# Stick-breaking prompt attention: the scores' second product with high queries and low keys alone, two query tiles at once in the two halves of the array's rows

## The reference, cut to what matters

```
z = einsum('bqhd,bkhd->bhqk', q, k) * scale          # scores, 64-long products
log_keep = where(causal, log_sigmoid(-z), 0)
after = sum of log_keep over the keys behind this one
a = exp(log_sigmoid(z) + after), 0 where not causal
o = einsum('bhqk,bkhd->bqhd', a, v)
```

## Time and profile before

| | |
|---|---|
| median of 3 executions | 2858.61 us (2857.3 to 2861.83) |
| profiled execution, span from first to last instruction (what is shown of its own time) | 2862.5 us |
| busy: PE, DVE, ACT, POOL | 2813.8, 1649.9, 1317.5, 1155.7 us |
| stage `phase_attend` on TensorE, scores | 1453.6 to 2555.6 us |
| mean granted TensorE clock | 0.992 of full |

### The profile page before, as it was taken

How to read it: one execution, slowest core, us unless ns; L and a number is a source line. 1 busy time by engine, 2 the same in 40 slices (tenths; PEclk the granted TensorE clock), 3 DMA queues, 4 the chain that set the end, 5 groups by cost and what they waited for, 6 DMA issues and landing times. The chain is left out here.

```text
span 2862.5 us, 42044 instructions
## 1 busy us (share of the span) xinstructions
PE 2813.8 (98%) x14856; PEld 2467.1 (86%) x14856; DVE 1649.9 (58%) x2151; ACT 1317.5 (46%) x2733; POOL 1155.7 (40%) x1023
## 2 busy tenths in 40 slices
PE   7999999999999999999999999999999999999998
PEld 6999999999988888889978888888888888878886
DVE  5322132213243350112268999999999999988775
ACT  6000000000043331111157888888888888875542
POOL 3333333333110120002256867676777768651110
PEclk9999999999999999999999999999999999999999
DMA  5101111111064343434687766867767776767873
GB/s 157 38 23 37 38 38 30 32 41 38 13 200 130 122 167 143 169 120 147 186 245 211 228 197 200 243 198 215 220 203 211 237 198 196 218 187 211 238 219 108
DMA packets 280359, 433.33 MB, mean 151 GB/s; under 512 B 52578, under 2 KB 218594, under 8 KB 274180
## 3 DMA queue, kind: packets, MB, share of 16 engines
q1 hardware_dynamic: 269156, 391.41, 45.1%
q0 software_dynamic: 11040, 39.86, 4.7%
HBM read 307.40 MB, written 123.81 MB: 151 GB/s over the span
## 5 line engine op out<-in xcount | busy, mean ns | idle before, releaser
L1981 POOL TENSOR_TENSOR a_a<-a_a,a_prod 128x512 f32<-128x512 f32 (+3 forms) x640 | 661.6, 1049 | 305.3 <-DVE a_prod L1932 183.8
L1932 DVE TENSOR_TENSOR_SCAN a_prod<-a_keep,a_prod,a_restart 128x513 f32<-128x513 f32 x384 | 476.0, 1268 | 30.2 <-ACT a_keep L1876 28.9
L1875 ACT ACTIVATE a_a<-a_pz 128x512 f32<-128x512 f32 (+3 forms) x640 | 358.0, 559 | 58.2 <-PE a_pz L1802 51.6
L1885 ACT ACTIVATE a_ath<-a_pt 128x512 fp32r<-128x512 f32 (+3 forms) x640 | 327.3, 556 | 102.2 <-PE a_po L1816 72.7
L1942 DVE TENSOR_TENSOR a_atl<-a_pt,a_ath 128x512 fp32r<-128x512 f32 (+3 forms) x640 | 359.9, 597 | 18.5 <-ACT a_ath L1885 16.1
L1876 ACT ACTIVATE a_keep<-a_pz 128x512 f32<-128x512 f32 (+3 forms) x640 | 361.6, 566 | 0.0
L1825 PE MATMUL a_pt<-ident,a_a 128*128 128x128 f32 x2176 | 316.9, 275 | 4.5 <-DVE a_atl L1942 2.4
L1825 PEld LDWEIGHTS a_pt<-ident,a_a 128*128 128x128 f32 x2176 | 262.2, 142 | 44.4 <-DVE a_atl L1942 5.0
L1801 PE MATMUL a_pz<-a_kh,a_q 128*128 128x512 f32 (+3 forms) x640 | 255.9, 403 | 3.5 <-ACTq L1866 2.0
L279 POOL TENSOR_TENSOR w_wh<-w_raw,w_gain 128x1024 fp32r<-128x1024 f32 x22 | 41.5, 1889 | 537.0 <-PE v_pg L349 279.9
L1814 PE MATMUL a_po<-a_ath,a_v 128*128 128x512 f32 (+3 forms) x640 | 245.9, 388 | 1.6 <-POOL a_v L1992 0.9
(11 more groups left out here) (233 smaller groups left out, 6165.1 us busy)
## 6 DMA issues: line engine op xcount, KB each, us to landing
a_x<-x_d SPq DMA_DIRECT2D x84, 896.0 KB, 5.7
a_x<-x_d SPq DMA_DIRECT2D x56, 832.0 KB, 4.9
a_kh<-kh_t SPq DMA_DIRECT2D x32, 512.0 KB, 7.0
a_kl<-kl_t SPq DMA_DIRECT2D x32, 512.0 KB, 9.1
w_raw<-in_a_w_in POOLq DMA_DIRECT2D x30, 512.0 KB, 4.8
x<-f_xn POOLq DMA_DIRECT2D x17, 512.0 KB, 5.3
g_y_in<-sz_t SPq DMA_DIRECT2D x17, 512.0 KB, 7.4
g_x<-x SPq DMA_DIRECT2D x17, 512.0 KB, 3.7
```

What stands on the lines that cost most here:

```text
L1875: act.activation(a[:, s, q, 0:w], pz[:, n % ZS, 0:w], ACT.Sigmoid, scale=SCALE)
L1885: act.activation(ath[:, b % AS, c0:], pt[:, turn_slot(pr, hh, b), c0:], ACT.Copy).then_inc(at_hi, 1)
L1932: dve.tensor_tensor_scan(prod[:, s, 0:w + 1][:, ::-1], keep[:, n % KS, 0:w + 1][:, ::-1], restart[:, 0:1].broadcast_to([P, w + 1]), prod[: ...
L1981: pool.tensor_tensor(part, part, prod[:, n % PS, after:after + w], ALU.mult).then_inc(weighted, 1)
```

## The change

For an even query tile only the first product is made at its turn. At the odd tile's turn come its first product and then the second products of both tiles, with 64 rows each: qh of the even tile by kl in one half of the rows, qh of the odd tile by kl in the other. ql·kl is no longer computed. Since both need qh, and `q2` has qh in one half only, a new tile `qx` holds qh of the odd query tiles in the other half; for odd heads the halves of `q2` and `kl2` change places. `qx` is loaded by one more DMA per head (`load_odd`), for the first head at the beginning of the stage on a semaphore of its own. `prod` goes from 8 slots to 6, its slots now count through all pieces, and each scan waits for the scan two pieces before it. The planner's costs follow.

```diff
-ZS, TS, US, KS, PS, AS = 2, 3, 4, 4, 8, 4
+ZS, TS, US, KS, PS, AS = 2, 3, 4, 4, 6, 4
+def half_of(hh):
+    return slice(hh * HD, (hh + 1) * HD)
+def score_time(n):
+    return pe_time(piece_width(n)) * (2 if n % 2 else 1)
-        self.whole = sum(2 * pe_time(piece_width(n)) for _, n in self.pieces)
+        self.whole = sum(score_time(n) for _, n in self.pieces)
-                return 2 * pe_time(w), 0.249 + 0.000469 * w - pe_time(w)
+                return score_time(self.pieces[k][1]), 0.249 + 0.000469 * w - pe_time(w)
             line.append((what, *divmod(h, 2), n))
+            if what == "score" and n % 2 == 0:
+                return
+            if what == "score":
+                at[what, k - 1] = end
-            self.move(ready, 2, ("queries", *divmod(h, 2), 0), 2, 1.05, ("queries", h + 2))
+            self.move(ready, 2, ("queries", *divmod(h, 2), 0), 3, 1.31, ("queries", h + 2))
+        qx = sb("a_qx", [P, QT // 2, P], F32R)
-                for dst, top, bottom in sources:
-                    for part, src in ((slice(0, HD), top), (slice(HD, P), bottom)):
+                for dst, first, second in sources:
+                    for part, src in ((half_of(hh), first), (half_of(1 - hh), second)):
                         sp.dma_start(dst[hh][part, :].bitcast(F32), src[rows, 0:SEQ]).then_inc(qk_loaded[hh], 16)
+                    if dst is q2:
+                        load_odd(2 * pr + hh, qk_loaded[hh])
+            def load_odd(h, loaded):
+                odd = qh_t[bass.ds(h * HD, HD), 0:SEQ].rearrange("d (i two p) -> d i two p", two=2, p=P)[:, :, 1, :]
+                sp.dma_start(qx[half_of(1 - h % 2), :, :].bitcast(F32), odd).then_inc(loaded, 16)
             queries, high_keys, low_keys = ((q2, qh_t, ql_t),), ((kh2, kh_t, kh_t),), ((kl2, kl_t, kl_t),)
+            load_odd(0, odd_loaded)
             sp.wait_ge(early.x_stored, 16 * 4 * KT)
             load_x(0, 0)
                     if n == 0:
                         pe.wait_ge(early.first_loaded, 96)
+                        pe.wait_ge(odd_loaded, 16)
                 elif n == 0:
-                    pe.wait_ge(qk_loaded[hh], 96 * (pr + hh))
+                    pe.wait_ge(qk_loaded[hh], 112 * (pr + hh))
                 pe.matmul(o, lhs, kh2[hh][:, p0:p0 + w], start=True, stop=False)
-                pe.matmul(o, lhs, kl2[hh][:, p0:p0 + w], start=False, stop=True).then_inc(z_ready, 1)
+                if q % 2:
+                    even, odd = half_of(hh), half_of(1 - hh)
+                    w0 = piece_width(n - 1)
+                    pe.matmul(pz[:, (n - 1) % ZS, 0:w0], q2[hh][even, (i - 1) * P:i * P], kl2[hh][even, p0:p0 + w0],
+                              start=False, stop=True).then_inc(z_ready, 1)
+                    pe.matmul(o, qx[odd, i // 2, :], kl2[hh][odd, p0:p0 + w],
+                              start=False, stop=True).then_inc(z_ready, 1)
-                w, s = piece_width(n), n % PS
+                w, s = piece_width(n), piece(pr, hh, n) % PS
                 dve.wait_ge(weighted, piece(pr, hh, n - PS) + 1 + N_PIECE)
+                dve.wait_ge(scanned, piece(pr, hh, n - 2) + 1 + N_PIECE)
-                    dve.wait_ge(scanned, piece(pr, hh, n - QG) + 1 + N_PIECE)
```

More of the change, by code:

```diff
@@ L1625, in phase_attend @@
         passed, passed_sp, q_rest = sem("a_passed"), sem("a_passed_sp"), sem("a_q_rest")
+        odd_loaded = sem("a_odd_loaded")
         qk_loaded, v_loaded = sem2("a_qk_loaded"), sem2("a_v_loaded")
@@ L1933, in score @@
                                            restart[:, 0:1].broadcast_to([P, w + 1]),
-                                           prod[:, (n - QG) % PS, before:before + 1],
+                                           prod[:, (piece(pr, hh, n) - QG) % PS, before:before + 1],
                                            ALU.mult, ALU.bypass).then_inc(scanned, 1)
@@ L1980, in score @@
                 pool.wait_ge(scanned, piece(pr, hh, n) + 1 + N_PIECE)
-                pool.tensor_tensor(part, part, prod[:, n % PS, after:after + w], ALU.mult).then_inc(weighted, 1)
+                pool.tensor_tensor(part, part, prod[:, piece(pr, hh, n) % PS, after:after + w], ALU.mult).then_inc(weighted, 1)
             def split_v(pr, hh):
```

## The result

The changed kernel takes 2947.0 us (2946.1 to 2951.5) against 2860.2 us of the kernel before beside it: ratio 1.0305, 95% interval 1.029 to 1.0319, 87 us slower. The forecast was 2820 us, faster; the range ended at 2885. One of the rivals, the drain, had the sign and the place; its 2902 us were too few, most of all because it booked nothing for the pairing itself.

The account below looks back on a forecast made before the run. TensorE was taken as the bound (busy 98% of the span), VectorE 6.7% behind in the attention stage's window. From 2858.6 us, -56 + 14 + 3.5 = -38.5 gave 2820 us; range 2798 to 2885, the likeliest case's own 2798 to 2838.

Parts of the forecast that it names:

- the drain: Before and behind each pair, TensorE drains at changes between 128 and 64 rows: 0.16 us each, 2902 us; chance 0.26.
- TensorE's term, -56 us: Second products of 320 pairs: halves fully overlap, saving 62 us, less 6 us for narrow pairs' loads: minus 56 us.
- The 6 us for the loads of narrow pairs: At the 64 pairs of 128 with 256 columns, two weight loads aren't covered: some 0.1 us lost each.
- up to 2920 if weight loads also wait: Upper end of the drain rival at the row changes on TensorE: 2920 us instead of 2902.
- Loads one ahead: In pairs on TensorE, weight loads begin only one matmul ahead: 27 us saved instead of 56, 2835 us; chance 0.15.
- ScalarE's bursts: ScalarE has no sigmoid for 0.6 us per pair, filled with other work: zero, bound 0 to 25 us.
- VectorE, booked at 14 us: In the attention stage VectorE becomes late next, keeping about 3% idle: 14 of the 56 us lost.
- First load 3.5 us: At the start of the stage the first score waits for head 0's load_odd: plus 3.5 us.
- Later loads: 15 more DMAs of 256 KB for the later heads, issued a head ahead into SP's waiting: zero.
- 6 slots of `prod`: VectorE's waits for GpSimd with fewer slots of prod: zero, bound 0 to 5 us.

Follow-up runs that it names:

- all_but_pairs: The changed kernel without pairs: both products at once over 128 rows, lists drawn up for that; qx loads, exchanged halves, 6 slots stay; 2864.9 us, ratio 1.0020.
- early_release: pair_full with the same lists, but each piece makes both products at once and gives its slot away; 2880.1 us, ratio 1.0066.
- pair_full: The changed kernel, but a pair's two second products use all 128 rows, one after the other; 2892.0 us, ratio 1.0114.
- half_alone: The kernel before, with every second product over 64 rows, alone, right behind the first; 3084.6 us, ratio 1.0791.
- single halves: The kernel before with lone 64-row second products: at every piece (half_alone, 3084.6 us) or at the odd tiles only (2969.6 us).
- changed_3_and_2: The changed kernel with three PSUM slots for scores and two banks for transposes; 2928.6 us, ratio 1.0239.
- same_half: The changed kernel, with the odd tile's second product in the same half of the rows as the even tile's; 2994.1 us, ratio 1.0468.
- slots_3_and_2: pair_full without the loads of qx, with a third PSUM slot for scores taken from the transposes, restart left in PSUM; 2867.1 us, ratio 1.0024.
- prod6_padded: The kernel before with only 6 of the 8 slots of prod in use and the wait for the scan two before; 2860.5 us, ratio 1.0001.
- three_slots_single: The kernel before (single pieces, 128 rows, no qx) with three PSUM slots for scores and restart moved to SBUF; 3097.7 us, ratio 1.0836.

## Why the prediction was wrong

The loss taken apart, each step the difference of two ratios times 2860 us:

| step | us |
|---|---|
| before to all_but_pairs: loads of qx, 6 slots, exchanged halves | +6 |
| to early_release: lists drawn up for pairs | +13 |
| to pair_full: even slot given away with the odd one | +14 |
| to the changed kernel: row changes less overlap | +55 |

By the intervals of the ratios each step is good to 1 to 2 us (the first) or some 5 to 7 us (the others), and in another order the shares could differ. They add up to 88, against 87 measured.

**TensorE's term, -56 us.** This is the step that failed: measured +55. The overlap itself was as forecast: pairs start together, and the wider member alone counts (62 us forecast, 63 in the starts, 47 in the kernel's time). The argument that the pitch goes by the columns that stream, and that the halves share nothing, was right inside the pair and silent on its borders, and the borders cost 117 us by the starts. The 6 us for the loads of narrow pairs were not there: a 128/256 pair takes 0.312 us to the next start (median), a lone 256 in half_alone 0.310. I took the lower end of an unknown from an argument on what two instructions share, when the unknown was what a third one pays.

**The drain rival.** It named the place (before and behind each pair) and the sign; its chance was 0.26. Its price was 0.16 us per change, 102 in all, from the modelled end of a matmul. Measured by the starts is 0.18 per change in the mean, of another make: 0.09 of stall and 0.06 to 0.105 of a weight load that cannot run ahead. Of the 320 pairs 189 stand before transposes (0.34 per in-and-out) and 131 before something else (0.39), together 117 us; less 63 that is 54, against a measured 55. The single halves cost a little less in the kernel's time (0.352 and 0.339) than the same sum gives for their neighbours (0.37 and 0.38), and why stays open. My "up to 2920 if weight loads also wait" came near for TensorE (changed_3_and_2, without most of the slots' cost, stands at 2929). The Trainium skill (TensorEngine Tiling (Array Packing), Key Properties) says that changing the tiling mode drains TensorE; the trace agrees, 0.33 and 0.43 us in place of 0.23. I had held the transposes with 18 columns of weights against it. They are no counterexample: there the columns of the weights changed, and here the rows do.

**Loads one ahead.** This rival was wrong: both loads of a pair start together. The Trainium skill (TensorE: Matmul & The Clock Gate, Part 3) has loads overlap where the row group differs and starts 4 ns apart; the trace shows 3 ns. In same_half, where the half is the same, the loads start 0.11 and the matmuls 0.34 apart.

**ScalarE's bursts, booked at nothing.** The second failure: 27 us with the lists (bound 0 to 25). I had filled the 0.6 us per pair with ScalarE's other work by the sum. But its list is fixed, and a slot that comes late holds up what stands behind it: in pair_full TensorE waits 10.7 us for slots and is busy 888 of the 900 us, with no row change at all. The size of ScalarE's idle share did not protect it; with a third slot 22 us of the cost went (slots_3_and_2).

**VectorE, booked at 14 us.** Never reached, as TensorE only became slower.

**First load 3.5 us:** measured 3.6. The first score came 4.1 us after SP issued the load (1450.26 to 1454.32), and before the change 0.5 us after SP's first issue. **Later loads, 6 slots of `prod`:** for the slots nothing that could be measured (prod6_padded); the loads are within the 6 us of the first step.

## What to carry to other kernels

Running two 64-row matmuls beside each other works, but going from 128 rows to 64 and back costs 0.34 to 0.39 us here, more than the 0.23 us that one stream of 512 columns saves. So count borders and not matmuls. By these numbers two pairs of 512 columns in one in-and-out would save 0.46 us for at most 0.39; that is an estimate, and no run here tried it. It would need four slots filled at once. And before two producers are tied into one hand-over, count the buffers: with two slots both belong to the same pair, and the one that fills them waits for the one that empties them.

## What the runs showed of the hardware beyond that

The product scan with its second operand in PSUM and the same scan with all operands in SBUF differ by more than a third: 1268 ns against 1734 ns (1779 in three_slots_single), with GpSimd's multiplies slowed from 1211 to 1657 ns at the same time; with the third slot that came along, the two kernels lost 224 and 238 us. The Trainium skill (SBUF — State Buffer, Who interferes with whom) says that a VectorE instruction with two inputs in SBUF contends with a GpSimd instruction that reads SBUF; both engines' means agree with that (slots_3_and_2 has a third slot with `restart` left in PSUM and stands at 2867 us). A 64-row product streams no faster than one of 128 rows: in half_alone the median distance from it to the next start is 0.43, 0.37, 0.31 and 0.25 us for 512, 384, 256 and 128 columns, 0.06 for every 128 columns, the same slope as with 128 rows on top of a fixed 0.2.
